# A two-block transformer kernel on one core: weights in pieces, products and vector steps in another order in five phases

## The chip, the cores and the metric

The program runs on one core of one Trainium2 chip. The metric is the device time of one execution in microseconds. Each engine of the core (TensorE or PE, VectorE or DVE, ScalarE or ACT, GpSimd or POOL) has its own instruction stream, and SyncE (SP) issues the DMA transfers. The streams meet only at semaphores. All data is float32. The trace has two rows for each float32 `matmul` of the code, while the listings of instruction order have one.

## The reference, cut to what matters

Two blocks are computed one after the other on 512 latent and 256 context tokens of width 1024. The first has two layers, each a mixer, a projection with a residual, and a gated feed-forward of width 2816. The second has a mixer of two branches and, at the end, a mixture of 16 experts in which each expert chooses its 64 tokens:

```python
m_lat = jnp.split((sc @ mod_w[l] + mod_b[l])[:, None, :], 6, axis=-1)      # modulation of a layer
h_lat = _modulate(_rms(x_lat, norm_pre_mix[l]), m_lat[0], m_lat[1])
...
x_lat = x_lat + m_lat[2] * _rms(o_lat @ w_out, norm_post_mix[l])           # the closing of a mixer
h_lat = _modulate(_rms(x_lat, norm_pre_ffn[l]), m_lat[3], m_lat[4])
x_lat = x_lat + m_lat[5] * _rms(_swiglu(h_lat, ...), norm_post_ffn[l])     # the tail of a feed-forward
...
affinity = jax.nn.softmax((h @ router_w).astype(F32), axis=-1)             # expert_choice_moe, 512 x 16
gate, idx = lax.top_k(jnp.swapaxes(affinity, 1, 2), cap)                   # cap = 64
xe = jax.vmap(lambda hb, ib: hb[ib])(h, idx)
hid = jax.nn.silu(xe @ w_gate) * (xe @ w_up)                               # for each expert, width 1408
ye = hid @ w_down * gate                                                   # added back at idx
```

## The kernel before

The program is a chain of phases. Each is a `Block` with its own semaphores, and each ends with a barrier over all engines, so nothing of a phase starts before the last instruction of the one ahead. Two things cross a barrier: data, and the object `Ahead`, a small buffer (`first`) into which the phase ahead has already loaded the first rows of the next phase's weights. Tokens come in six tiles of 128, two of context and four latent ones.

`opening` normalises and turns the six tiles and computes the first four blocks (of 512 columns) of layer 0's modulation. SP loads the tokens, the four blocks of weights of 2 MB each (line 236) and the tables (line 241). TensorE waits for each block and does 32 small products (8 slices `k`, 4 groups of columns; line 268). VectorE adds the bias (line 322), SP stores the result to memory (line 244) and loads it back as columns (lines 247 and 248), and then ScalarE and VectorE modulate all tiles.

`closing` runs three times: as `out0` (six tiles, weights ahead), `out1` (four tiles, none ahead) and `wo` (four tiles, weights ahead). It multiplies all tiles with weights in two jobs of 512 columns and eight slices `k`, then gates, adds to the residual, normalises and turns. Its unit is a tile of a job, summed over `k` in one bank of PSUM. Six banks are used in turn, and a unit beyond the sixth waits for `yg_done`. For job 0, slices 0 and 1 are in `ahead.tile`; slices 2 and 3, and then 4 to 7, are loaded at the start of the phase (`firsts`, line 402), and the first tile waits for each (`first_in`).

`down` (the second half of both feed-forwards) makes its products in pairs of tiles; the normalisation of a finished pair lies beside the next pair's products. For the last pair there is no next one, and its steps stand alone: ScalarE squares `y` (line 1068), VectorE takes the mean (`mean_y`), gates `y` (line 1158), takes the reciprocal (1160) and adds to `x` (`residual`, line 1163), ScalarE squares `x` (1077), VectorE takes the mean (`mean_x`) and scales (`normed`, lines 1173 and 1175), TensorE turns (line 1010), and ScalarE and VectorE (`take`) write the result.

`route` computes the logits (line 4284), the softmax and its transpose, and eight rounds of maximum search (lines 4329 and 4330) that mark each expert's 64 tokens in `taken`. A token's rank among those of its expert is a product with a triangle (`UPTO`) for its own tile and with ones for each tile before it (line 4300). From the ranks, VectorE writes `pick`, a 0/1 matrix of 512 tokens by 16 x 64 slots (line 4342). While this runs, SP fills the ring `experts_ring` with the first expert weights.

`experts` gathers the chosen tokens as products with `pick` (line 4409), by groups of 256 slots, that is four experts. Group 0 comes first, before anything else; the others are gathered as fillers between the products of a pair of experts. Line 4478 is the gate and up products, line 4511 the down products, line 4422 the scatter. Each piece of the ring that TensorE has used is released, and SP then loads the next piece into it (line 4636). VectorE begins the phase with the modulation (line 4544), waits for the row `gate` (line 4391), and multiplies `pick` with the gates (line 4559), which TensorE then turns (line 4417).

## Time and profile before

| what | us |
|---|---|
| runs of the kernel before | 4405.62, 4415.44, 4419.54 |
| their median | 4415.44 |
| the profiled execution, as timed | 4411.0 |
| its span in the trace | 4409.2 |
| TensorE busy | 4042.8 (92%) |
| VectorE busy | 1666.8 (38%) |
| ScalarE busy | 881.9 (20%) |
| GpSimd busy | 743.6 (17%) |

The span goes from the first to the last instruction in the trace; the time as measured has 1.8 us more around it. A line such as L465 names a line of the kernel. PE stands for products, PEld for the loading of the stationary operand, and SPq for the issue of transfers by SP. The granted clock (PEclk) is given as a share of 2.4 GHz, so 0.50 is 1.2 GHz. In the trace the parts of a tile's name before the first underscore are shortened: `out` is out0 and out1, `ffn_down` both layers.

### The profile page before, as it was taken

Reading aid. Unit: us, or ns where it says so; the run is one execution under the profiler, and the core shown is the slowest. Engines: PE = TensorE matmul, PEld = TensorE weight load, DVE = VectorE, ACT = ScalarE, POOL = GpSimd, SP = SyncE. Lnnn points to the kernel's source line nnn. Section 1 sums busy time; section 2 is a strip of 40 time slices with the busy share of each in tenths; the row PEclk is TensorE's granted clock in tenths of the full one; section 3 lists DMA queues with packets and bytes.
Section 4 is the critical chain, followed back from the end, with each engine's and each line's share of the span. In section 5 each row is a group of like instructions: output and inputs, shape, how many; then the busy total and the mean of one; then the engine's idle time right before and its main releaser. Section 6 shows DMA issues by size and latency. Waiting matters only on the chain. (4 is left out here: it accounts for less than half of the span.)

```text
span 4409.2 us, 46565 instructions
## 1 busy us (share of the span) xinstructions
PE 4042.8 (92%) x18631; PEld 2449.3 (56%) x18631; DVE 1666.8 (38%) x2942; ACT 881.9 (20%) x1666; POOL 743.6 (17%) x505
## 2 busy tenths in 40 slices
PE   7997889999989998899988999989998897999988
PEld 4664445554446765588546777775554445433433
DVE  2346342225724453433555566550024223111111
ACT  3124320000122333200013333321022211000000
POOL 0003212223411111123323333320002200000000
PEclk8999999999999999999999999999998997999999
DMA  4117511114421101353441000004200223899998
GB/s 167 39 43 261 169 40 64 64 43 148 170 84 29 53 29 59 117 209 116 144 117 29 22 27 20 17 32 142 70 1 1 108 84 126 361 421 421 422 421 369
DMA packets 317021, 579.68 MB, mean 131 GB/s; under 512 B 55836, under 2 KB 186108, under 8 KB 316168
## 3 DMA queue, kind: packets, MB, share of 16 engines
q1 hardware_dynamic: 316808, 576.70, 35.4%
q8 instruction: 150, 2.46, 0.2%
q14 instruction: 63, 0.52, 0.0%
HBM read 566.02 MB, written 10.63 MB: 131 GB/s over the span
## 5 line engine op out<-in xcount | busy, mean ns | idle before, releaser
L2951 PE MATMUL dn_ps<-room,dn_w 128*128 128x512 f32 (+1 forms) x616 | 226.1, 520 | 4.8 <-DVE dn_qx L3470 2.5
L764 PE MATMUL ffn_up_ps<-room,ffn_up_w 128*128 128x384 f32 (+1 forms) x704 | 209.0, 441 | 12.4 <-DMA ffn_up_w<-in_ffn_w_gate 12.4
L764 PE MATMUL ffn_up_ps<-ffn_up_t,room 128*128 128x384 f32 (+1 forms) x704 | 205.7, 436 | 0.8 <-DVE room L844 0.8
L764 PE MATMUL ffn_up_ps<-room 128*128 128x384 f32 (+1 forms) x704 | 203.9, 432 | 0.0
L4478 PE MATMUL experts_ps<-experts_ring,experts_xs 128*64 128x512 f32 (+1 forms) x768 | 165.3, 582 | 27.8 <-DMA experts_ring<-in_w_up 27.8
L2374 PE MATMUL hgrn_ps<-room,hgrn_w 128*128 128x512 f32 x384 | 175.2, 597 | 0.0
L764 PEld LDWEIGHTS ffn_up_ps<-room,ffn_up_w 128*128 128x128 f32 x704 | 135.2, 193 | 71.7 <-DMA ffn_up_w<-in_ffn_w_gate 13.2
L4478 PE MATMUL experts_ps<-experts_ring,room 128*64 128x512 f32 (+1 forms) x768 | 160.7, 570 | 8.7 <-DMA experts_ring<-in_w_up 8.1
L2951 PEld LDWEIGHTS dn_ps<-room,dn_w 128*128 128x128 f32 x616 | 116.3, 194 | 94.2 <-issue 81.7
L764 PEld LDWEIGHTS ffn_up_ps<-ffn_up_t,room 128*128 128x128 f32 x704 | 134.8, 192 | 57.6 <-DVE room L844 1.7
L4511 PE MATMUL experts_ps<-experts_ring,experts_hidT 128*64 128x512 f32 x704 | 155.0, 594 | 11.6 <-issue 6.9
L764 PEld LDWEIGHTS ffn_up_ps<-room 128*128 128x128 f32 x704 | 133.8, 190 | 55.7
L1039 PE MATMUL ffn_down_ps<-ffn_down_w_sums,ffn_down_hid_sums 128*128 128x512 f32 x330 | 161.7, 599 | 2.3 <-DVE ffn_down_w_sums L1127 2.3
L4554 DVE TENSOR_TENSOR x_sb<-x_sb,experts_ps 128x512 f32<-128x512 f32 x64 | 44.0, 688 | 300.3 <-PE experts_ps L4422 300.3
L851 DVE TENSOR_TENSOR room<-ffn_up_ps,room 128x384 f32<-128x384 f32 (+1 forms) x154 | 73.4, 489 | 222.2 <-PE ffn_up_ps L764 222.2
L3314 POOL TENSOR_TENSOR dn_LT<-dn_W,cst 128x768 f32<-128x768 f32 x48 | 90.6, 1887 | 340.6 <-DVE dn_W L3396 329.0
L2371 PE MATMUL hgrn_ps<-hgrn_w,room 128*128 128x384 f32 (+1 forms) x456 | 138.9, 453 | 3.1 <-DMA hgrn_w<-in_odd_w_in 3.1
L465 PE MATMUL out_ps<-out_w,room 128*128 128x512 f32 x296 | 134.4, 610 | 7.4 <-DMA out_w<-in_even_w_out 6.6
L4478 PEld LDWEIGHTS experts_ps<-experts_ring,experts_xs 128*64 128x64 f32 x768 | 59.1, 142 | 134.9 <-issue 131.7
L1039 PE MATMUL ffn_down_ps<-ffn_down_w,ffn_hid 128*128 128x512 f32 x220 | 116.3, 611 | 15.5 <-DMA ffn_down_w<-in_ffn_w_down 14.8
L822 POOL TENSOR_TENSOR room<-ffn_up_w 128x512 f32<-128x512 f32 x44 | 56.8, 1290 | 419.1 <-PE ffn_up_ps L764 233.0
L175 PE MATMUL in_ps<-in_w,room 128*128 128x512 f32 (+1 forms) x296 | 119.9, 565 | 0.3 <-DMA in_w<-in_w_in 0.3
(626 smaller groups left out, 7204.5 us busy)
## 6 DMA issues: line engine op xcount, KB each, us to landing
experts_ring<-in_w_gate SPq DMA_DIRECT2D x128, 704.0 KB, 15.8
experts_ring<-in_w_up SPq DMA_DIRECT2D x128, 704.0 KB, 17.8
experts_ring<-in_w_down SPq DMA_DIRECT2D x160, 512.0 KB, 14.5
ffn_down_w<-in_ffn_w_down SPq DMA_DIRECT2D x55, 1024.0 KB, 4.7
att_wm<-in_mod_w SPq DMA_DIRECT2D x20, 2048.0 KB, 8.9
ffn_up_wm<-in_ada_w SPq DMA_DIRECT2D x12, 2048.0 KB, 12.3
ffn_up_w<-in_ffn_w_up SPq DMA_DIRECT2D x22, 1024.0 KB, 7.7
ffn_up_w<-in_ffn_w_gate SPq DMA_DIRECT2D x20, 1024.0 KB, 5.3
```

What stands on the lines that cost most here:

```text
L175: mm = nc.tensor.matmul(ps[:, u % 8, 0:wd], xT[:, k, t * P:(t + 1) * P], ahead.tile[:, k, 0:wd] if j == 0 and k < n_ahead else wt[:, j % r ...
L465: mm = nc.tensor.matmul(ps[:, u % BANKS, 0:wd], xT[:, k, t * P:(t + 1) * P], ahead.tile[:, k, 0:wd] if j == 0 and k < n_ahead else wt[:, j ...
L764: mm = nc.tensor.matmul(result(n, p), lhs[:, k, :], rhs[:, k, :], start=k == 0, stop=k == half - 1)
L822: nc.gpsimd.tensor_tensor(s[:, 0, :, :], quarter(n, 1, lo), quarter(n, 1, hi), ALU.add).then_inc(S["s1_done"], 1)
L851: nc.vector.tensor_tensor(kept(n, to), result(n, p), kept(n, q), ALU.add).then_inc(done, 1)
L1039: mm = nc.tensor.matmul(result(p, prod), lhs, rhs, start=j == 0, stop=j == STEPS - 1)
L2371: mm = nc.tensor.matmul(ps[:, bank, 0:b - a], hT[:, k, t * P:(t + 1) * P], ahead.tile[:, k, :] if j == 0 and k < n_ahead else wt[:, s, k, ...
L2374: mm = nc.tensor.matmul(ps[:, bank, :], wt[:, s, k, piece * P:(piece + 1) * P], hT[:, k, CTX:], start=k == 0, stop=k == KD - 1)
L2951: mm = nc.tensor.matmul(out, ahead.tile[:, k, :] if k < by_ahead else wt[:, h % 2, piece, k, :], hT[:, k, tok], start=k == 0, stop=k == KD ...
L3314: nc.gpsimd.tensor_tensor(LT[:, :, :], W[:, h % 2, :, :], over_chunks(HALVES + n + 1), ALU.mult).then_inc(S["lt_done"], 1)
L4478: mm = nc.tensor.matmul(ps[out_rows, 3 * n + c, 0:b - a], xs_now[:, j, at:at + SLOTS], ring[:, w_at + a:w_at + b], start=j == 0, stop=j == ...
L4511: mm = nc.tensor.matmul(ps[out_rows, 6 + half, :], hidT[:, f, out_rows], ring[:, w_at:w_at + 512], start=f == 0, stop=f == FT - 1)
```

## The change

Five places change.

1. `opening` loads its last block of weights as four pieces of two slices `k`, each with its own semaphore, and TensorE waits for each piece where it needs it.
2. `closing` with weights ahead does the products of the slices at hand for all tiles first, into one bank for each tile, and then goes through the tiles with the remaining slices.
3. `down` interleaves the steps of its last two tiles on VectorE. The gating is now a function `gated` of its own; in the earlier pairs it is called right ahead of `residual`, as it stood.
4. `route` computes the ranks in four products in place of ten. The triangle is multiplied with `taken` of all four tiles at once, and the ones with `taken` of tiles 0 to 2, 0 to 1 and 0, each summed into the columns of the tiles behind.
5. `route` writes only the slots of group 0 (256 columns for each tile) of `pick`. The other 768 columns are written at the start of `experts`, behind VectorE's wait for the row `gate`; `slot` lives longer for it. VectorE's gating of a tile waits for `picked`, and so does TensorE ahead of the first gather of group 1.

```diff
@@ opening, SyncE and TensorE
             for b in range(blocks):
-                sp.dma_start(wt[:, b, :, :], mod.w[:, :, bass.ts(mod.b0 + b, 512)]).then_inc(S["w_in"][b], 16)
+                if b < blocks - 1:
+                    sp.dma_start(wt[:, b, :, :], mod.w[:, :, bass.ts(mod.b0 + b, 512)]).then_inc(S["w_in"][b], 16)
+                else:
+                    for n, (k0, k1) in enumerate(PIECES_OF_LAST):
+                        sp.dma_start(wt[:, b, k0:k1, :], mod.w[:, k0:k1, bass.ts(mod.b0 + b, 512)]).then_inc(S["last_in"][n], 16)
...
                 for k in range(KD):
+                    for n, (k0, k1) in enumerate(PIECES_OF_LAST):
+                        if b == blocks - 1 and k == k0:
+                            pe.wait_ge(S["last_in"][n], 16)
@@ closing, TensorE
+            if ahead:
+                wd = jobs[0][2]
+                pe.wait_ge(ahead.sem, 16)
+                for i, t in enumerate(tiles):
+                    for k in range(n_ahead):
+                        nc.tensor.matmul(ps[:, i, 0:wd], xT[:, k, t * P:(t + 1) * P], ahead.tile[:, k, 0:wd], start=k == 0, stop=False)
             for j, (v, c, wd, units) in enumerate(jobs):
...
-                    for k in range(kt):
+                    for k in range(0 if j else n_ahead, kt):
@@ down, VectorE, the end
-            last = finished_beside(n_pairs)
-            for t in last:
-                mean_y(t)
-            for t in last:
-                residual(t)
-            for t in last:
-                mean_x(t)
-                normed(t)
-            for t in last:
-                take(n_pairs, t)
+            one, other = finished_beside(n_pairs)
+            mean_y(one)
+            gated(one)
+            mean_y(other)
+            residual(one)
+            gated(other)
+            mean_x(one)
+            residual(other)
+            normed(one)
+            mean_x(other)
+            normed(other)
+            take(n_pairs, one)
+            take(n_pairs, other)
@@ route, TensorE and VectorE
-            for m in range(tiles):
-                for before in range(m + 1):
-                    mm = nc.tensor.matmul(ps[:, 3, m * E:(m + 1) * E], cst[:, UPTO[0], :] if before == m else ones, taken[:, before, :],
-                                          start=before == 0, stop=before == m)
+            flat = taken[:, :, :].rearrange("p m e -> p (m e)")
+            for later in range(tiles):
+                mm = nc.tensor.matmul(ps[:, 3, later * E:tiles * E], ones if later else cst[:, UPTO[0], :], flat[:, 0:(tiles - later) * E], start=later == 0, stop=later == tiles - 1)
...
-                by_slot = pick[:, m, :].rearrange("p (e s) -> p e s", e=E)
-                nc.vector.tensor_tensor(by_slot, ...
+                picks(nc, pick, slot, slot_iota, m, 0, GROUP)
+GROUP = 2 * P // SLOTS
@@ experts, TensorE
                     if what == "gather":
+                        if of == 1 and i == 0:
+                            pe.wait_ge(S["picked"], tiles)
@@ experts, VectorE
             dve.wait_ge(S["gate_in"], 16)
...
+            for m in range(tiles):
+                picks(nc, pick, slot, slot_iota, m, GROUP, EXPERTS).then_inc(S["picked"], 1)
+
             def gate_slots(m):
+                dve.wait_ge(S["picked"], m + 1)
```

On TensorE at the start of the closing `out0`, one row for each product (`first` is the buffer with the weights loaded ahead, `out_w` the weights loaded in the phase). Before:

```order
L465 MATMUL out_ps<-first,room 128x512 [waits first_odd_in]
L465 MATMUL out_ps<-first,room 128x512
L465 MATMUL out_ps<-out_w,room 128x512 [waits out0_first_in0]
L465 MATMUL out_ps<-out_w,room 128x512
L465 MATMUL out_ps<-out_w,room 128x512 [waits out0_first_in1]
L465 MATMUL out_ps<-out_w,room 128x512 x3
L465 MATMUL out_ps<-first,room 128x512 x2
L465 MATMUL out_ps<-out_w,room 128x512 x6
```

In the changed kernel:

```order
L460 MATMUL out_ps<-first,room 128x512 [waits first_odd_in]
L460 MATMUL out_ps<-first,room 128x512 x11
L478 MATMUL out_ps<-out_w,room 128x512 [waits out0_first_in0]
L478 MATMUL out_ps<-out_w,room 128x512
L478 MATMUL out_ps<-out_w,room 128x512 [waits out0_first_in1]
L478 MATMUL out_ps<-out_w,room 128x512 x33
```

Ten more products on `first` now stand ahead of the first wait for weights of the phase.

On VectorE from the end of `route` into `experts` (`slot_iota_sb` holds the slot numbers, `first` now holds the row `gate`, and `room` is where the gated picks go). Before:

```order
L4342 TENSOR_TENSOR pick<-slot_iota_sb,route_slot 128x1024 x3
L44 UNCONDITIONAL_BRANCH
L4541 UNCONDITIONAL_BRANCH [waits barrier_Pool_Activation_PE_DVE_SP_release]
L4544 SCALAR_TENSOR_TENSOR experts_mul<-experts_cols 128x8 [waits n0_ident_in0]
L4559 TENSOR_TENSOR room<-pick,gates 128x1024 [waits n0_cond_in0]
```

In the changed kernel:

```order
L4367 TENSOR_TENSOR pick<-slot_iota_sb,slot 128x256 x3
L44 UNCONDITIONAL_BRANCH
L4568 UNCONDITIONAL_BRANCH [waits barrier_Pool_Activation_PE_DVE_SP_release]
L4571 SCALAR_TENSOR_TENSOR experts_mul<-experts_cols 128x8 [waits n0_ident_in0]
L4367 TENSOR_TENSOR pick<-slot_iota_sb,slot 128x768 [waits n0_cond_in0]
L4367 TENSOR_TENSOR pick<-slot_iota_sb,slot 128x768 x3
```

Three quarters of the columns moved from ahead of the barrier to behind it. (A semaphore's number is used again by later phases, so the names in the brackets are those of its first user.)

## Rows read from the trace of the kernel before

**Rows 1.** The chain that ended last, from the page: shares by engine.
```profile
PE 10%; DMA 3%; SPq 2%; issue 0%; DVE 0%; ACT 0%; DVEq 0%
```

**Rows 2.** Timeline of the opening: start us, length us, engine, line, operation, [idle before].
```profile
29.95 2.62 PE L268 MATMUL n_ps<-n_w,conditions 128*2 128x128 f32 x64 [3.16 <-DMA n_w<-in_mod_w]
...
35.00 3.30 PE L268 MATMUL n_ps<-n_w,conditions 128*2 128x128 f32 x64 [2.43 <-DMA n_w<-in_mod_w]
...
39.59 1.18 SPq L244 DMA_DIRECT2D mod<-n_mod  x4
```

**Rows 3.** Transfers, 0 to 50 us: issues, KB each, us to landing.
```profile
cst<-in_tables SPq DMA_DIRECT2D x1, 1216.0 KB, 17.6
```

**Rows 4.** Timeline of TensorE at the start of the closing out0.
```profile
509.41 1.95 PE L465 MATMUL out_ps<-first,room 128*128 128x512 f32 x4 [1.10 <-PEq L47]
...
513.27 1.98 PE L465 MATMUL out_ps<-out_w,room 128*128 128x512 f32 x4 [1.91 <-DMA out_w<-in_even_w_out]
...
519.90 6.70 PE L465 MATMUL out_ps<-out_w,room 128*128 128x512 f32 x8 [4.64 <-DMA out_w<-in_even_w_out]
...
526.43 1.88 PE L465 MATMUL out_ps<-first,room 128*128 128x512 f32 x4
...
533.30 1.88 PE L465 MATMUL out_ps<-first,room 128*128 128x512 f32 x4
```

**Rows 5.** Stretches: length, busy time of five engines, granted clock, DMA share, GB/s.
```profile
519.90:523.00 3.10, 3.10 (x4) 1.50 (x5) 0.00 (x0) 0.00 (x0) 0.00 (x0) 0.50 1.06 371
...
2265.00:2275.00 10.00, 9.82 (x26) 4.24 (x24) 6.04 (x12) 0.59 (x1) 0.00 (x0) 1.00 0.00 1
```

**Rows 6.** Timeline of TensorE at the start of the closing wo.
```profile
3622.97 1.96 PE L465 MATMUL wo_ps<-first,room 128*128 128x512 f32 x4 [1.44 <-PEq L47]
...
3629.21 3.70 PE L465 MATMUL wo_ps<-wo_w,room 128*128 128x512 f32 x8 [0.99 <-DMA wo_w<-in_w_o]
...
3632.75 1.88 PE L465 MATMUL wo_ps<-first,room 128*128 128x512 f32 x4
```

**Rows 7.** Timeline of the tail of `down`, second feed-forward.
```profile
2277.77 0.15 DVE L1154 TENSOR_SCALAR first<-first 128x1 f32<-128x1 f32 x1 [1.31 <-ACT room L1068]
...
2279.16 1.28 DVE L1163 SCALAR_TENSOR_TENSOR x_sb<-room,first,x_sb 128x1024 f32<-128x1024 f32 x1
...
2280.37 1.22 DVE L1158 TENSOR_TENSOR room<-room,ffn_down_gate 128x1024 f32<-128x1024 f32 x1
...
2283.51 0.75 DVE L1175 TENSOR_SCALAR room<-x_sb,first 128x1024 f32<-128x1024 f32 x1
...
2284.41 3.31 PE L1010 MATMUL ffn_down_ps<-cst,room 128*128 128x128 f32 x16 [9.59 <-DVE room L1175]
```

**Rows 8.** Timeline of the routing phase.
```profile
3692.68 13.81 PE L4284 MATMUL route_ps<-first,room 128*128 128x16 f32 x64 [2.31 <-PEq L47]
...
3708.24 1.01 PE L4290 MATMUL route_ps<-cst_small,gates 128*16 128x128 f32 x4 [1.75 <-DVE gates L4324]
...
3727.89 0.22 DVE L4338 TENSOR_TENSOR route_slot<-route_ps,route_taken 128x64 f32<-128x64 f32 x1 [4.62 <-PE route_ps L4300]
...
3728.38 4.63 DVE L4342 TENSOR_TENSOR pick<-slot_iota_sb,route_slot 128x1024 f32<-128x1024 f32 x4
```

**Rows 9.** Timeline of the first feed-forward's `down`, one operation of VectorE.
```profile
1138.74 0.42 DVE L1117 TENSOR_TENSOR ffn_down_hid_sums<-ffn_hid 128x256 f32<-128x256 f32 x1
```

**Rows 10.** Timeline of the start of the experts' phase.
```profile
3733.73 17.40 PE L4409 MATMUL experts_ps<-pick,room 128*128 128x256 f32 x64 [5.95 <-PEq L47]
...
3739.49 2.36 DVE L4559 TENSOR_TENSOR room<-pick,gates 128x1024 f32<-128x1024 f32 x2 [1.84 <-DMA first<-mod]
...
3756.75 0.33 SPq L4636 DMA_DIRECT2D experts_ring<-in_w_gate  x1
```

**Rows 11.** Transfers, 3690 to 3760 us: GB/s in 40 slices of 1.75 us, and one issue.
```profile
GB/s 0 0 139 128 409 422 431 415 431 422 428 418 428 425 425 422 425 425 425 425 418 100 0 0 0 14 21 279 2 0 0 0 0 0 0 0 0 0 61 328
...
first<-mod SPq DMA_DIRECT2D x1, 512.0 KB, 4.5
```

**Rows 12.** Transfers, 3760 to 4409 us: GB/s in 40 slices of 16.2 us.
```profile
GB/s 319 400 410 419 424 423 422 419 421 423 424 422 419 421 422 425 420 420 418 425 422 423 419 420 423 422 424 418 420 423 422 424 419 418 424 423 423 420 360 130
```

More of the change, by code:

```diff
@@ L464, in _ @@
                                 pe.wait_ge(S["first_in"][n], 16 * (len(v[k0 >= kt // 2]) if type(v) is tuple else 1))
-                        mm = nc.tensor.matmul(ps[:, u % BANKS, 0:wd], xT[:, k, t * P:(t + 1) * P], ahead.tile[:, k, 0:wd] if j == 0 and k < n_ahead else wt[:, j % ring, k, 0:wd], start=k == 0, stop=k == kt - 1)
+                        mm = nc.tensor.matmul(ps[:, u % BANKS, 0:wd], xT[:, k, t * P:(t + 1) * P], wt[:, j % ring, k, 0:wd], start=k == 0, stop=k == kt - 1)
                     mm.then_inc(S["mm_done"], 1)
@@ L4248, in quarter_tables, with route @@
     return {name: np.ascontiguousarray(t.astype(np.float32)) for name, t in tables.items()}
-def route(nc, tag, hT, I, cst, ones, slot_iota, pick, aff, work, load, places, ahead):
+def route(nc, tag, hT, I, cst, ones, slot_iota, slot, pick, aff, work, load, places, ahead):
     tiles = TILES - CTX_TILES
@@ L4340, in _, with picks, experts @@
             for m in range(tiles):
-                by_slot = pick[:, m, :].rearrange("p (e s) -> p e s", e=E)
-                nc.vector.tensor_tensor(by_slot, slot_iota[:, 0:SLOTS].unsqueeze(1).broadcast_to([P, E, SLOTS]),
-                                        slot[:, m, :].unsqueeze(2).broadcast_to([P, E, SLOTS]), ALU.is_equal)
-def experts(nc, tag, x, x_hat, pick, aff, gated, pick_gateT, gain, mod, w_gate, w_up, w_down, ident, ring, load, piece_in, places, pool, xs, hid, hidT, gate, out):
+                picks(nc, pick, slot, slot_iota, m, 0, GROUP)
+GROUP = 2 * P // SLOTS
+def picks(nc, pick, slot, slot_iota, m, e0, e1):
+    shape = [P, e1 - e0, SLOTS]
+    return nc.vector.tensor_tensor(pick[:, m, e0 * SLOTS:e1 * SLOTS].rearrange("p (e s) -> p e s", s=SLOTS), slot_iota[:, 0:SLOTS].unsqueeze(1).broadcast_to(shape),
+                                   slot[:, m, e0:e1].unsqueeze(2).broadcast_to(shape), ALU.is_equal)
+def experts(nc, tag, x, x_hat, slot, slot_iota, pick, aff, gated, pick_gateT, gain, mod, w_gate, w_up, w_down, ident, ring, load, piece_in, places, pool, xs, hid, hidT, gate, out):
     F, FT = EXPERT_FF, EXPERT_FF // P
@@ L4383, in experts @@
         phase(nc, tag, "cols_in", "gate_in", "mul_done", "piece_used", "up_mm", "silu_done", "hid_done", "turned", "hid_turned", "down_mm", "out_done",
[L4384 removed]
+              "gather_mm", "gather_out", "picked", "gated_done", "pick_turned", "pick_taken", "scatter_mm", "scatter_out", "stored") as (block, S),
     ):
```

21 lines of the change are left out of this document (11 added, 10 removed).

## The prediction

> **What bounds the kernel now.** I read four views in this order. The chain that ended last covers 15% of the span, which is the experts' phase alone (from 3733 us on): 10% is TensorE and 5% transfers of the ring and their issue [rows 1]. The transfers move 418 to 425 GB/s in every full slice from 3809 us to 4376 us [rows 12], so that stage goes by its transfers, and what it costs as a whole is fixed by bytes. What is not fixed is when it begins. Before 3733 us the program is a row of phases with a barrier behind each, so a microsecond taken from the path inside a phase is a microsecond of the span, unless something inside that phase is then late. So I read, second, the timelines of the five places that the change touches and looked for what the last instruction of each phase had waited for; third, the granted clock of TensorE there; fourth, the transfers around the routing phase. All sums are against the profiled execution: 4409.2 us span, 4411.0 us as timed. That is 4.4 us under the median of 4415.4 us, so the predicted time is the median less the gain.
>
> **Opening.** The last 2 MB of weights land at 35.00 us, 5.05 us behind the third block, and only then do 32 products run (64 rows of the trace, two for each float32 product) in 3.30 us [rows 2]. In four pieces the first three land some 1.25, 2.5 and 3.8 us behind the third block's and are used before the last lands, for 16 rows of the trace need at most 0.83 us. Left behind 35.00 us is one piece, 3.30 / 4 = 0.83 us. Saved: 2.5 us. What could be late next is the table load. It is queued right behind these weights with 1216 KB [rows 3]; at the rate of the weights (2 MB in 5.05 us) it needs 3.0 us and lands at 38.0 us. It used to be done when the modulation was stored at 39.59 us [rows 2]. The stores now start 2.5 us earlier, at 37.1 us, and overlap its last microsecond. I take 0.1 us off for that: 2.4 us, between 1.6 (the stores wait for all of the table) and 2.5.
>
> **Closing of layer 0 (out0).** TensorE does four trace rows on the weights loaded ahead, waits, does four on the first piece, waits 4.64 us for the second, and does the next eight in 6.7 us at a granted clock of 0.50, which is 1.2 GHz [rows 4, 5]. Tile 0 takes 526.43 - 509.41 = 17.02 us; tile 1, with nothing to wait for, takes 533.30 - 526.43 = 6.87 us, or 0.429 us a row. The loss is 10.15 us. In the changed kernel 24 rows on the weights at hand come first and take 24 x 0.429 = 10.3 us, to 519.7 us. The first piece landed by 513.27 us and is at hand. Its four rows end at 521.4 us, and the second piece landed by 519.90 us. Neither wait is left, and TensorE is busy all the while, so I take the clock to stay at 2.4 GHz. What is next late? Tile 0's product ends at about 525 us instead of 526.4; job 1 starts at 550.6 instead of 560.8 us and needs the bank of tile 0, free by 528 us, and weights issued before 521 us. Nothing. Saved: 10.1 us. The bounds: 6.9 us if the eight rows still run at 1.2 GHz (then 3.2 us stays lost), 10.2 at most.
>
> **Closing of block 2 (wo).** The same with four tiles: 3632.75 - 3622.97 = 9.78 us for tile 0 against 6.87 [rows 6], a loss of 2.9 us. The 16 rows on weights at hand take 6.9 us, to 3629.9 us; the second piece landed by 3629.21 us. Saved: 2.9 us, bounds 2.3 (the two waits alone) and 2.9. The third closing (out1) has nothing loaded ahead and does not change.
>
> **Tail of `down`, in both feed-forwards.** VectorE's order is now by dependence rather than by kind. In the profile of before, VectorE stands idle for 1.31 us until ScalarE's second square is done, at 2277.77 us, and only then gates the first tile (1.22 us, as the second's at 2280.37); the first normalised tile starts at 2283.51 [rows 7]. Now the first gating lies in that idle stretch, from 2276.5 us. The first residual starts at 2278.0, the second gating at 2279.2, ScalarE's square of the first x at 2279.4, and the second residual at 2280.8. The first normalised tile starts at 2282.2, which is 1.3 us earlier; the second is 1.0 us earlier. TensorE's 16 transposes start at 2284.41 [rows 7] and then run without a gap worth naming, so the first tile sets the end. I take 1.2 us each, 2.4 us for two, with bounds 1.6 and 2.6. The cover here is VectorE's idle stretch; if ScalarE's square were quicker, the gating would be on the path again.
>
> **Routing.** Ranks: VectorE waits 4.62 us for 20 trace rows of TensorE [rows 8]. The 64 logit rows of the same phase and width take 13.81 / 64 = 0.216 us each, so the 20 are 4.3 us of it, and 0.3 us is fixed. Now there are eight rows, with 64, 48, 32 and 16 columns. The wider ones are new; four transposes of the same phase move 128 columns and take 1.01 / 4 = 0.25 us a row, which bounds them. I take 8 x 0.216 = 1.7 us. Saved: 2.6 us, bounds 2.3 and 2.6. Picks: four operations of 1024 columns take 4.63 us [rows 8]. Four of 256 columns remain: at least 4.63 / 16 = 0.29 us each by columns, at most 0.42 us as a 128x256 operation in `down` lasts [rows 9]. I take 0.35, 1.4 us together. Saved: 3.2 us, bounds 2.95 and 3.5. The gather and with it the whole ring schedule start 5.8 us earlier.
>
> The other 768 columns go to the start of the experts' phase, behind the wait for the gate, which ended 5.8 us into that phase [rows 10]: 4 x 0.87 = 3.5 us (three quarters of 4.63), over 9.3 us in. Queued behind them on VectorE is the gating of the picks for the transposes, which TensorE takes up only after its first gather of group 1. TensorE's own new wait stands at that gather, which begins with the first release of the ring at 3756.75 us, 23 us in [rows 10]. So the added work lies beside other work with 13 us to spare. Without that cover it would cost 3.5 us.
>
> **Sum.** 2.4 + 10.1 + 2.9 + 2.4 + 5.8 = 23.6 us. 4411.0 - 23.6 = 4387.4 us against the profiled execution, 4391.8 us against the median: 4392 us, ratio 0.9947. With all low bounds it is 17.7 us, with all high ones 24.3.
>
> **Two rules against the trace.** In the profile of before, transfers of 512 and 704 KB in the ring keep about 422 GB/s as long as several are queued [rows 11, 12]. The Trainium skill, "DMA: Bandwidth & Descriptors", section "Bandwidth", asks instead for transfers of 1 MiB and more and gives about three quarters of peak at that size; by an estimate from its fit (2 us fixed and bytes over 436 GB/s), three more transfers would cost 6 us if they stood one behind the other, and the opening would lose 3.5 us. The trace disagrees for queued transfers; no run so far shows it in the opening. Second, in `down` TensorE changes its PSUM bank after every two trace rows for a whole stage at a granted clock of 1.00 [rows 5]. The Trainium skill, "TensorE: Matmul & The Clock Gate", section "A second HAM failure mode: psum-queue depth-cycling", warns that cycling through banks each iteration can make the clock swing. The new loop in out0 changes banks after every four rows, so by the rule the clock could fall there; the trace speaks against it.
>
> **Rivals.**
> (a) *The routing's gain is taken back by the ring.* If the transfers of the experts' stage were already under way without a break, starting TensorE earlier would move nothing: 4392 + 5.8 = 4398 us. Against it: the rate falls to 0 at about 3728 us, with the ring full, and rises only when the first pieces are released at 3756.75 us [rows 10, 11]. The release moves with the gather.
> (b) *The clock stays low in out0* while the banks are cycled: 24 + 12 rows at twice 0.429 us cost 15 us more, which leaves a gain of 8 us: 4407 us. Against it is the stretch of `down` [rows 5].
> (c) *The opening's pieces run one behind another.* A 512 KB load of the gate row lands 4.5 us after its issue [rows 11]; four of them in a row would need 18 us instead of 5: 4392 + 13 = 4405 us. The Trainium skill's fit above is the mild form of this rival. Against it is the queued rate.
> (d) *Slower: the new wait on `picked` stalls the ring.* If the gate's load were queued behind ring pieces, VectorE would come late to the 768 columns, TensorE would stand at the first gather of group 1, and with it every release behind it. It costs nothing up to 23 us into the phase, and a microsecond for each one after that; it eats the whole gain from 23 + 23.6 = 46.6 us on, where I work out 9.3. Picks that end 60 us in would give 4392 + 37 = 4429 us. What speaks for it is only that the phase now starts at 3727.9 us, within a microsecond of the ring's last first-fill piece.
> (e) *The change doesn't do what it says* at one place (a wait that I take as gone has another cause, out0's being the large one): 4392 + 6 = 4398 us.
>
> **Chances.** Forecast 0.78; (a) 0.06; (b) 0.03; (c) 0.02; (d) 0.03; (e) 0.08. The runs of before spread from 4405.6 to 4419.5 us, so a median of three may be 5 us off by itself, about as much as the bounds of the sum leave open. Forecast alone: 4385 to 4400 us. With (a), (e) and half of the rest: 4381 to 4404 us. About 0.3% (13 us) is what a measurement of this kernel can tell from no change: faster by more than that is 0.86 (forecast, (a), (e), less the noise), within it 0.11 ((b), (c) and noise), slower 0.03 ((d)).
>
> **What would show it.** In the changed profile: out0's first 24 rows without a gap and clock 1.00 throughout job 0, tile 0 ending near 525 us less the opening's 2.4; the opening's last block in four groups of products, 0.8 us of them behind the last landing; the rank products within 2 us; the experts' first gather 5.8 us earlier relative to the routing's start, and the first ring release 23 us after it as before; no wait of TensorE on VectorE's picks. The prediction is wrong if TensorE's clock is low in out0, if the ring's rate in the experts' stage is not the one of before, or if the stage's length from gather to end is not the same.

## The result, and the profile after

| what | before | changed |
|---|---|---|
| median, us | 4415.29 | 4390.03 |
| runs, us | 4405.62 to 4419.54 (4) | 4389.81 to 4390.7 (4) |
| ratio of the runs, 95% interval | | 0.9946 (0.9929 to 0.9963) |
| the profiled execution, as timed | 4411.0 | 4390.07 |
| its span | 4409.2 | 4388.3 |
| TensorE busy | 4042.8 | 4037.8 |

The changed kernel is faster by 25.3 us by the medians and by 23.8 us by the means, where 23.6 us had been forecast; the ratio in the table is that of the means. Between the two profiled executions it is 20.9 us. The rest of this document compares traces, and so explains the 20.9 us. The difference to 25.3 comes from where the two profiled executions stand among their runs: the one of the kernel before is 4.3 us under its median, and the one of the changed kernel is on its median.

*The page.* The chain that ended last has the same makeup as in [rows 1], and the experts' stage moves data at the same rate as in [rows 12]. Shares by engine, and GB/s from 3739 to 4388 us in 40 slices:

```profile
PE 11%; DMA 3%; SPq 1%; issue 0%; DVE 0%; ACT 0%; DVEq 0%
...
GB/s 312 403 416 419 425 422 423 419 421 422 424 422 418 421 422 424 421 420 420 422 423 424 419 419 423 426 421 420 418 423 424 423 419 419 423 424 422 420 348 129
```

*Opening.* Timeline of the changed kernel, to set beside [rows 2]. The last column is the idle time ahead of the group and what ended it.

```profile
29.92 4.91 PE L277 MATMUL n_ps<-n_w,conditions 128*2 128x128 f32 x112 [4.06 <-DMA n_w<-in_mod_w]
...
35.01 0.62 PE L277 MATMUL n_ps<-n_w,conditions 128*2 128x128 f32 x16 [0.18 <-DMA n_w<-in_mod_w]
...
36.91 1.18 SPq L249 DMA_DIRECT2D mod<-n_mod  x4
```

The third block (64 rows) and three of the four pieces (48 rows) now form one group of 112, with no gap that the trace sets apart. One piece of 16 rows is left behind the last landing at 35.01 us. The four pieces land in the time of the one transfer (35.00 us before). The store is issued 2.68 us earlier.

*Closing of layer 0.* TensorE, as [rows 4]:

```profile
508.95 10.54 PE L460 MATMUL out_ps<-first,room 128*128 128x512 f32 x24 [1.10 <-PEq L47]
519.32 51.23 PE L478 MATMUL out_ps<-out_w,room 128*128 128x512 f32 x119
```

Both waits are gone: 119 rows follow on the 24 without a gap. The granted clock is 1.00 over both jobs; the one stretch at 0.50 in this phase begins at 600.7 us, when they are done. Three stretches (length, PE busy, clock, DMA share, GB/s):

```profile
505.00:515.00 10.00, 8.23 (x30) 1.00 0.50 122
515.00:520.00 5.00, 5.00 (x13) 1.00 1.03 272
520.00:525.00 5.00, 5.00 (x13) 1.00 1.09 367
```

*Closing of block 2.* TensorE from the end of the phase ahead, as [rows 6], and below it a stretch with the same columns:

```profile
3605.76 0.66 PE L4160 MATMUL mix_ps<-cst,mix_sum 128*128 128x128 f32 x4 [1.07 <-DVE mix_sum L4248]
3607.86 8.80 PE L460 MATMUL wo_ps<-first,room 128*128 128x512 f32 x16 [1.44 <-PEq L47]
3616.49 8.75 PE L478 MATMUL wo_ps<-wo_w,room 128*128 128x512 f32 x20
...
3608.20:3611.20 3.00, 3.00 (x4) 0.50 0.75 253
```

Here too the waits are gone, but 16 rows take 8.80 us instead of 6.9: for some 3 us the granted clock is 0.50.

*Tail of `down`, second feed-forward*, as [rows 7]:

```profile
2268.57 0.15 DVE L1167 TENSOR_SCALAR first<-first 128x1 f32<-128x1 f32 x1 [0.62 <-ACT room L1081]
2268.64 1.21 DVE L1170 TENSOR_TENSOR room<-room,ffn_down_gate 128x1024 f32<-128x1024 f32 x1
...
2271.49 1.22 DVE L1170 TENSOR_TENSOR room<-room,ffn_down_gate 128x1024 f32<-128x1024 f32 x1
...
2274.44 0.75 DVE L1190 TENSOR_SCALAR room<-x_sb,first 128x1024 f32<-128x1024 f32 x1
...
2275.34 3.65 PE L1023 MATMUL ffn_down_ps<-cst,room 128*128 128x128 f32 x16 [8.27 <-DVE room L1190]
```

TensorE's idle time ahead of the transposes falls from 9.59 to 8.27 us, 1.3 us less. The first gating lies directly behind the first mean, in what was idle time.

*Routing*, as [rows 8]:

```profile
3691.95 1.01 PE L4308 MATMUL route_ps<-cst_small,gates 128*16 128x128 f32 x4 [1.75 <-DVE gates L4341]
...
3707.03 0.69 PE L4318 MATMUL route_ps<-route_taken,cst_small 128*128 128x64 f32 x2 [0.32 <-DVE route_taken L4350]
...
3707.51 1.41 PE L4318 MATMUL route_ps<-route_taken,ones_sb 128*128 128x48 f32 x6
3709.03 0.23 DVE L4355 TENSOR_TENSOR slot<-route_ps,route_taken 128x64 f32<-128x64 f32 x1 [2.06 <-PE route_ps L4318]
...
3709.52 1.43 DVE L4367 TENSOR_TENSOR pick<-slot_iota_sb,slot 128x256 f32<-128x256 f32 x4
```

VectorE waits 2.06 us for the ranks instead of 4.62, and its picks take 1.43 us instead of 4.63: 2.56 and 3.20 us.

*Start of the experts' phase*, as [rows 10]:

```profile
3711.68 17.95 PE L4434 MATMUL experts_ps<-pick,room 128*128 128x256 f32 x64 [2.76 <-PEq L47]
...
3716.64 3.56 DVE L4367 TENSOR_TENSOR pick<-slot_iota_sb,slot 128x768 f32<-128x768 f32 x4 [2.31 <-DMA first<-mod]
...
3735.16 4.21 PE L4434 MATMUL experts_ps<-pick,room 128*128 128x256 f32 x16
3735.25 0.33 SPq L4667 DMA_DIRECT2D experts_ring<-in_w_gate  x1
```

The 768 columns are done at 3720.2 us, 8.5 us behind the start of the first gather. TensorE's first gather of group 1, 15 us later, has no idle time ahead of it. The first release is 23.6 us behind the first gather (23.0 before).

### The profile page after: what moved, and what is told of

It reads as the page before. It is cut to its first block and busy times, and to the rows that moved or that the text cites. A ratio compares the mean times of both kernels' runs of the same rounds, so it can differ in the third digit from the quotient of the medians.

```text
span 4388.3 us, 46552 instructions
## 1 busy us (share of the span) xinstructions
PE 4037.8 (92%) x18619; PEld 2443.9 (56%) x18619; DVE 1668.8 (38%) x2946; ACT 882.0 (20%) x1666; POOL 743.0 (17%) x505
```

## The experiments

Each phase ends with a barrier, so the traces can be compared phase by phase. The table stands for all that follows. It gives the length of a phase from barrier to barrier in us, and in brackets how much of it lies at a granted clock of 0.50. The numbers are worked out from the barrier ends and clock records of each trace.

```
phase          before      before      parts 1 to 4 of the change alone            changed kernel
                           again       opening    ahead      tail       route      first      again      third
opening       49.4(18)    49.9(17)    47.1(13)   49.6(17)   50.7(18)   49.4(18)   46.7(16)   47.9(15)   46.7(13)
att, block 0 198.4(38)   200.4(41)   202.0(44)  198.0(38)  198.0(38)  203.1(51)  201.1(44)  201.1(44)  197.4(34)
out0         107.2(12)   105.3(10)   106.7(12)   97.1( 6)  104.8( 9)  106.5(15)   97.1( 5)   97.1( 5)   97.1( 5)
down0        227.4(21)   226.9(21)   227.3(21)  227.0(21)  225.8(17)  227.3(21)  226.0(17)  226.1(17)  226.0(17)
hgrn         483.6(13)   483.4(16)   483.6(17)  483.3(16)  484.7(17)  483.6(17)  484.7(17)  484.9(17)  484.8(17)
out1          94.3(22)    94.2(22)    94.4(22)   97.7(29)   98.2(32)   94.2(22)   98.2(32)   94.6(25)   98.1(32)
down1        161.2(21)   161.3(21)   161.4(23)  161.2(21)  160.2(21)  161.2(21)  160.9(21)  160.0(21)  159.8(21)
dn           709.8(40)   706.6(33)   709.5(41)  703.7(24)  707.6(37)  703.7(24)  708.1(36)  707.5(37)  707.6(36)
mla          364.2(64)   360.4(53)   363.4(60)  363.2(59)  360.5(53)  363.2(59)  360.2(53)  360.2(53)  360.2(53)
mix          127.0( 3)   127.1( 3)   127.0( 3)  125.7( 0)  127.1( 3)  127.0( 3)  125.9( 0)  127.1( 3)  127.0( 3)
wo            69.7( 6)    69.7( 6)    69.7( 6)   68.5(10)   69.6( 6)   69.7( 6)   68.5( 7)   66.8( 6)   66.8( 6)
route         41.1(41)    41.1(41)    41.1(41)   41.1(41)   41.1(41)   35.3(35)   35.3(35)   35.3(35)   35.3(35)
experts      675.5(30)   676.3(39)   677.1(25)  676.1(31)  675.8(32)  675.3(27)  676.6(38)  677.7(37)  677.0(42)
all phases  4408.9      4401.1      4409.9     4391.2     4403.8     4400.1     4387.9     4387.0     4384.1
```

(The four phases left out, `gla`, `up0`, `up1` and `in2`, stay within 1.7 us of each other over all nine.)

### One part of the change alone

Each kernel is the one before with the lines of one part of the diff shown ahead of the prediction: part 1; part 2; part 3; parts 4 and 5.

> The kernel before with the opening's last weights in pieces and nothing else. My theory: the opening ends 2.7 us earlier (46.7 instead of 49.4 us, as in the changed kernel), and the phases whose code is the same move by up to 4 us each, up or down, because the granted clock falls at other places in them; so the total is 2.7 us less, give or take 5: 4407 to 4417 us against 4415. Rival, parts add up exactly and the other phases stay put: every phase behind the opening has its length of before to 0.3 us and the total is 4412.6 us.

Measured: 4405.55 us (4403.68 to 4415.56, 10 runs), ratio 1.0 (0.9991 to 1.001). The opening is 47.1 us long, against 49.4 to 50.7 in the five traces with the old one: at least 2.3 us less. Part of that spread is the landing itself, for the last weights land between 34.8 and 36.1 us in those five and at 35.33 us here. From the first product on the last weights to the end of the phase it is 14.7 to 14.9 us in the five and 12.0 us here, so 2.6 to 2.9 us less. The rival, that the other phases stay put to 0.3 us, is refuted: `att` is 3.6 us longer and `mla` 0.8 us shorter.

> The kernel before with the products on the weights at hand first, in both closings. My theory: out0 is 10.1 us shorter in this run too, its 24 first rows at a granted clock of 1.00. In wo the changed kernel gave only 1.2 us because half of the 16 rows ran at 1.2 GHz; if that was where the clock happened to fall, wo gives 1.2 to 2.9 us here and its 16 first rows take 6.9 or up to 10.5 us. Rival: going from bank to bank brings the clock down, then the 16 rows of wo take 8.8 us here too, and the 24 rows of out0 show a low clock in some part. Total 4400 to 4407 us by either.

Measured: 4397.58 us (4390.5 to 4405.16, 9 runs), ratio 0.9981 (0.9971 to 0.999). `out0` is 97.1 us long. The old one takes 104.8 to 107.2 in five traces, so the gain is 7.7 to 10.1 us. `wo` is 68.5 instead of 69.7, and its 16 first rows take 8.80 us: 1.2 us where 2.9 was forecast, as in the first trace of the changed kernel. That is half of the rival's sign; the other half, a low clock in the 24 rows of `out0`, is missing. The banks get a test of their own below.

> The kernel before with the interleaved tail of the last pair. My theory: from the first mean of y to the first product of the next phase 12.4 and 12.6 us instead of 13.9 and 13.6, so 2.5 us in all, and the total 2.5 us less, give or take the clock's 5: 4408 to 4418 us. Rival: the earlier transposes run at a lower clock and give the gain back, then the two stretches are 13.3 us or longer and the total does not move.

Measured: 4410.77 us (4401.75 to 4412.91, 10 runs), ratio 1.0006 (0.9996 to 1.0015). The interval reaches from 1.8 us less to 6.6 us more and does not contain the 2.5 us that were expected, though the two phases are shorter, by 1.1 to 1.6 and by 1.0 to 1.2 us.

> The kernel before with the ranks in four products and the picks by group. My theory: the routing phase is 35.3 us instead of 41.1, the first gather starts 5.8 us earlier and the experts' phase keeps its length of 675.5 us to 0.5, so the total is 5.8 us less, give or take the clock's 5 in earlier phases. Rival: the experts' phase takes some of it back, since it was 1.1 us longer in the changed kernel (676.6), then it is again 676.6 us here.

Measured: 4402.88 us (4396.52 to 4408.94, 10 runs), ratio 0.9993 (0.9984 to 1.0002). The routing is 35.3 us instead of 41.1, 5.8 as worked out, and the experts' phase has kept its length (675.3 against 675.5 to 677.1).

The kernel before has a median of 4407.39 us on that chip (4399.86 to 4416.89, 30 runs). The four differences of medians are 1.8, 9.8, -3.4 and 4.5 us, 12.7 together, while the changed kernel wins 25.3 and, below, 21.9. Each of the four has an interval of some 4 us to both sides, so the medians can't say what a part of 2 us is worth, and whether the missing 9 us are more than noise stays open. In the traces the parts do add up: over the phases that they touch, the four kernels are 2.3, 11.3, 2.6 and 5.8 us shorter than the first trace of the kernel before, 22.0 together, and the changed kernel in its first trace 21.5. What follows from these four runs is read phase by phase in the table.

*Where the tail's gain went.* One row of the table answers it. The phase behind the first feed-forward, `hgrn`, isn't touched by the diff. It takes 483.3 to 483.6 us in all five traces with the old tail and 484.7 to 484.9 in all four with the new one. Its first products on TensorE, in the kernel before:

```profile
1244.35 3.65 PE L1010 MATMUL ffn_down_ps<-cst,room 128*128 128x128 f32 x16 [9.59 <-DVE room L1175]
1250.19 2.90 PE L2371 MATMUL hgrn_ps<-first,room 128*128 128x384 f32 x4 [2.19 <-PEq L47]
1256.19 5.83 PE L2371 MATMUL hgrn_ps<-hgrn_w,room 128*128 128x384 f32 x12 [3.10 <-DMA hgrn_w<-in_odd_w_in]
```

And in the changed kernel:

```profile
1232.48 3.47 PE L1023 MATMUL ffn_down_ps<-cst,room 128*128 128x128 f32 x16 [8.27 <-DVE room L1190]
1238.13 2.02 PE L2390 MATMUL hgrn_ps<-first,room 128*128 128x384 f32 x4 [2.19 <-PEq L47]
1243.81 6.83 PE L2390 MATMUL hgrn_ps<-hgrn_w,room 128*128 128x384 f32 x12 [3.66 <-DMA hgrn_w<-in_odd_w_in]
```

The same 12 rows take 1.0 us more. The stretch around them stands at 0.72 before and at 0.50 after (length, busy time of five engines, clock, DMA share, GB/s; kernel before, then changed):

```profile
1254.80:1261.00 6.20, 4.81 (x10) 2.68 (x11) 1.65 (x10) 0.23 (x1) 0.00 (x0) 0.72 0.86 150
```

```profile
1242.80:1249.00 6.20, 5.19 (x8) 2.86 (x9) 1.65 (x10) 0.23 (x1) 0.00 (x0) 0.50 0.95 173
```

The clock records say when. In all five traces with the old tail TensorE stands at 0.50 when `hgrn` begins, and the last low stretch at its start ends 9.4 to 9.8 us into the phase. In all four with the new tail the clock is back at 1.00 across the barrier, falls 1.0 us into the phase and stays low until 11.2 to 11.4 us. The first 16 rows of `hgrn` are done 0.7 to 1.2 us later for it, counted from the phase's start, and some 0.4 us more are lost around a second low stretch, which begins at 71 us with the old tail and at 73 with the new one. Why the clock falls there at all with the new tail isn't shown.

`down0` and `hgrn` together are 710.3 to 711.0 us in the five traces with the old tail and 710.5 to 711.0 in the four with the new one. So the 1.1 to 1.6 us that the first tail wins are given back in the next phase, in the form of a later stretch at 1.2 GHz. Behind the second tail, `dn` moves by up to 6 us in traces with the same tail (703.7 to 709.8), so whether that gain survives can't be told.

### The same kernels again

> The changed kernel once more, beside runs of the kernel before on the same chip, and its trace. My theory (run-to-run spread comes from where the granted clock falls): its runs spread over some 15 us as those of the kernel before do, their median lies 17 to 25 us below it, and in the trace att0, out1, dn and mla, whose code is unchanged, differ from the first trace by 2 to 6 us each, each with its time at 1.2 GHz. Rival, the changed kernel is tied to one good alignment: 4390 us again within 1 us, and the same phase lengths to 0.3 us.

Measured: 4384.6 us (4383.82 to 4390.21, 5 runs) against 4406.45 (4399.25 to 4419.09, 11 runs), ratio 0.9953 (0.9937 to 0.9968): 21.9 us. `out0` and `route` are as in the first trace, `wo` is 66.8 us, and `out1`, which is the same code as before, falls back from 98.2 to 94.6. Of the four phases that I had named, only `out1` moved as expected; `att` and `mla` are the same to 0.1 us and `dn` differs by 0.6, and the runs spread over 6.4 us and not 15. So neither theory holds whole: phases do move between executions, but fewer than I thought. The 25.3 us of the first comparison also rest on four runs of the kernel before with a median of 4415.29 us, while the 41 later ones, beside the kernels of this section and the one ahead of it, have medians of 4407.39 and 4406.45.

> The changed kernel, unchanged, profiled a third time. Asked: is the last product of block 2 (68.5 us in the first trace, 66.8 us in the second) set by where the clock falls. If so, its 16 products between the turns take 7.1 us with the granted clock at 1.00 over them or 8.8 us with a stretch at 0.50, and the stage 66.8 or 68.5 us accordingly, nothing else. If the second trace was special for another reason, some third value. Query product of block 0 97.1 us and routing 35.3 us as in both traces; sum within 10 us of 4387 us.

> The kernel before, unchanged, profiled a second time. Asked: how far the stages of one and the same code move between two executions. If where the granted clock falls is drawn anew in each execution, single stages (attention of block 0, the query product of block 1, the network and attention of block 2) will stand 1 to 5 us from the first trace, each together with its own time at the 1.2 GHz level, with a sum within some 10 us of 4408.9 us; the stages with little time at 1.2 GHz within 0.5 us. If it follows from the code alone, each stage agrees with the first trace within 0.5 us. Of the changed places: query product of block 0 between 104.8 and 107.2 us, last product of block 2 69.7 us, routing 41.1 us.

Measured, on one chip: 4386.21 us, and 4403.19 us for the kernel before, 17.0 apart; one more run of the kernel before beside them took 4409.73 us, 23.5 above. In the third trace of the changed kernel the 16 rows of `wo` run at full clock:

```profile
3603.16 0.66 PE L4160 MATMUL mix_ps<-cst,mix_sum 128*128 128x128 f32 x4 [1.07 <-DVE mix_sum L4248]
3605.26 7.11 PE L460 MATMUL wo_ps<-first,room 128*128 128x512 f32 x16 [1.44 <-PEq L47]
...
3605.30:3612.00 6.70, 6.70 (x16) 3.08 (x17) 0.00 (x0) 0.00 (x0) 0.00 (x0) 1.00 0.85 303
```

The idle times ahead of them (1.07 and 1.44 us) are the same to the hundredth as in the first trace, where 8.80 us stood. Where the low stretch went is seen in the phase ahead, `mix`. Third trace:

```profile
3526.05 1.94 PE L4150 MATMUL mix_ps<-cst,room 128*128 128x128 f32 x8 [2.57 <-ACT mix_yT L4200]
...
3525.60:3529.00 3.40, 2.94 (x10) 2.44 (x11) 3.33 (x5) 1.97 (x4) 0.00 (x0) 0.51 0.00 0
```

First trace, at the same place of the phase:

```profile
3530.07 1.12 PE L4150 MATMUL mix_ps<-cst,room 128*128 128x128 f32 x8 [2.71 <-ACT mix_yT L4200]
...
3528.40:3531.80 3.40, 1.73 (x10) 1.30 (x11) 3.02 (x5) 2.23 (x5) 0.00 (x0) 1.00 0.00 0
```

In every one of the nine traces one stretch of 3.4 us at 0.50 lies either in `mix`, where it costs 1.1 to 1.4 us, or right at the start of `wo`, where TensorE is never idle and it costs 1.7. Over both phases the gain is 2.8 to 3.0 us in two traces of the changed kernel (193.9 and 193.8 against 196.7 and 196.8), and 2.3 in the first (194.4). What decides between the two places isn't shown.

The second trace of the kernel before moves the same way: `att` +2.0, `out0` -1.9, `dn` -3.2, `mla` -3.8 us, and 7.8 us in all, with not a letter of the code changed. `out1`, which I had expected to move as well, is the same to 0.1 us. With the old `out0`, the eight rows on the late weights are at 1.2 GHz for a longer or shorter part of their length. 6.70 us in [rows 4] is this in the second trace:

```profile
520.75 5.39 PE L465 MATMUL out_ps<-out_w,room 128*128 128x512 f32 x8 [4.06 <-DMA out_w<-in_even_w_out]
```

### Does changing the bank cost clock?

The loop over the weights at hand, with tiles and slices exchanged, so that the bank changes with each product instead of every second one:

```diff
-                for i, t in enumerate(tiles):
-                    for k in range(n_ahead):
+                for k in range(n_ahead):
+                    for i, t in enumerate(tiles):
```

> The changed kernel with the products on the weights at hand taken slice by slice instead of tile by tile, so that each one goes to another bank than the one before. The same products and sums. My theory: the granted clock follows what TensorE did before, not the banks: the 24 rows of out0 take 10.5 us again, the 16 of wo 6.9 to 10.5 us with the low part at their beginning. Rival (the Trainium skill, TensorE: Matmul & The Clock Gate, section A second HAM failure mode: psum-queue depth-cycling): changing banks lets the clock swing, then changing twice as often gives more of it: over 12 us for the 24 rows, over 9 us for the 16.

Measured: 4391.65 us (4386.17 to 4396.4, 7 runs), ratio 0.996 (0.9946 to 0.9974). `out0` is 97.1 us and `wo` 66.8 us long, as in the second and third trace of the changed kernel. The 24 rows of `out0` and the clock over them:

```profile
514.03 10.54 PE L460 MATMUL out_ps<-first,room 128*128 128x512 f32 x24 [1.10 <-PEq L47]
...
514.00:524.30 10.30, 10.27 (x24) 4.67 (x25) 0.00 (x0) 0.00 (x0) 0.00 (x0) 1.00 0.86 227
```

So neither the clock nor the length of these phases depends on how often the bank changes here. The rule of the Trainium skill that the prediction weighed ("TensorE: Matmul & The Clock Gate", section "A second HAM failure mode: psum-queue depth-cycling") isn't borne out at this place, and the bank isn't what made `wo` slow in the first trace. The page tells of a bfloat16 kernel whose TensorE idles briefly between groups of products; the 24 rows here are float32 and have no gap between them, so that case isn't tested.

The whole kernel was slower than the changed kernel beside it, by 7.0 us in the median and 4.4 in the mean, with ranges that overlap. Its trace is 2.7 us longer than the second one of the changed kernel, and 4.0 us of difference lie in `att` (205.1 us, 58 of them at 0.50, against 201.1), which runs ahead of the edited loop. Whether the rest is more than noise wasn't measured.

### Keeping TensorE busy

If low stretches give gains back, products whose results nobody reads might prevent them. The first kernel puts four behind the last two turns of `wo` and eight beside the maximum search of the routing; the second also puts seven of 384 columns into the tail of `down`:

```diff
+            for n in range(SLOTS // 8):
+                pe.wait_ge(S["own"], 4 + 2 * n)
+                nc.tensor.matmul(ps[:, 4, 0:BUSY], cst[:, IDENT, :], hT[:, 0, 0:BUSY], start=True, stop=True)
             pe.wait_ge(S["mask_done"], 1)
```

> The changed kernel with products whose results nobody reads: four in the idle stretches of TensorE at the end of wo, and eight of 512 columns beside the eight rounds of the maximum search. My theory: the routing runs at 1.2 GHz only because TensorE stood idle before it. With the idle filled, the 64 logit rows take 6.9 instead of 13.8 us, the ranks about 1 instead of 2.1, the first gather 16.6 instead of 17.9, and wo is not longer: routing 27 to 29 us instead of 35.3, total 7 to 9 us below the changed kernel. Rival: the logit rows are bound by their weight loads or by issue and not by the clock, then they stay at 13.8 us and nothing moves.

Measured: 4386.5 us (4382.88 to 4388.25, 4 runs), ratio 0.9953 (0.9936 to 0.997), the same as the changed kernel beside it. The routing is 33.6 us long, 1.7 less. I had expected 27 to 29 us, and 7 to 9 us off the total. The 64 logit rows, which I had expected at full clock, are not:

```profile
3673.43 13.06 PE L4314 MATMUL route_ps<-first,room 128*128 128x16 f32 x64 [1.45 <-PEq L47]
...
3673.40:3674.00 0.60, 0.57 (x6) 1.00 0.00 0
3674.00:3675.00 1.00, 1.00 (x8) 0.62 0.48 139
3675.00:3676.00 1.00, 1.00 (x6) 0.50 0.37 97
```

`wo` now has no low stretch at all, but the clock falls one microsecond into the logits, behind the 1.4 to 1.5 us of idle time at the barrier and with TensorE busy without a gap. The six rows at 1.00 take 0.1 us each and the later ones 0.2, so the rival is wrong too: it is the clock that the rows go by. What the fillers keep up is the end of the phase: VectorE waits 1.23 us for the ranks instead of 2.06. The first gather behind it takes 17.7 us, where 16.6 was expected.

> As before this, and seven more such products of 384 columns in each tail of down, each behind a step of VectorE or ScalarE. My theory: the 16 transposes of each tail take 1.9 instead of 3.5 us and the next phase starts at 2.4 GHz, 1.5 to 3 us a tail, so 3 to 6 us less than the kernel with the busy routing alone. Rival: the transposes wait for VectorE's second tile anyway, and the next phase waits for its weights; then it gains less than 1.5 us, or the added products hold the first transpose up.

Measured: 4386.91 us (4382.76 to 4391.68, 4 runs), ratio 0.9955 (0.9937 to 0.9973). `down0` is 224.8 us (226.0 to 226.5 without the fillers), with 10.2 us at 0.50 instead of 17.1. Its 16 transposes take 1.2 us for each eight, at full clock, but with a wait of 0.57 us for VectorE's second tile between them, as the rival had it. `hgrn` is 485.0 us: no less than in the changed kernel. The low stretch at its start is there all the same, and over the two phases the fillers bring about 1 us (709.8 against 710.5 to 711.0 in the three traces of the changed kernel and the one of its tail alone). The 24 rows of `out0` had a low stretch in this execution (12.23 us, phase 98.8), the only one of seven with the new loop. Neither version is measurably faster than the changed kernel.

## Why the prediction was right

| term | forecast, us | measured at its place | what became of it |
|---|---|---|---|
| opening | 2.4 | 2.7 (2.3 with this part alone) | kept, 1.5 in the second trace |
| `out0` | 10.1 | 10.1 against the first trace | 7.7 to 10.1 against five |
| `wo` | 2.9 | 1.2 | 2.9 in the other two traces |
| tails | 2.4 | 2.5 (1.5 and 1.0) | the first given back in `hgrn` |
| routing | 5.8 | 5.8 | kept |
| sum | 23.6 | 22.3 | 20.9 as timed |

**Opening, ranks and picks.** The three costs that were taken from rows of the trace came out within 0.3 us. Of the opening's 3.30 us, 0.62 is left rather than 0.83, because that piece ran at a granted clock of 1.00, while the clock was 0.57 over the 3.30 us. The 0.1 us for the table load was not needed: the store is issued as soon as the bias is added. In the second trace of the changed kernel the pieces' products run at 1.2 GHz, one behind another without a gap, and the phase takes 47.9 us; there the cover is thinner than I worked out, and the gain is 1.5 us against the first trace of the kernel before.

**`out0`.** The step held as written: 24 rows in 10.54 us, no wait, full clock. The gain was sized on one execution, however. The old phase depends on how much of the eight rows behind its 4 us wait is at 1.2 GHz, and the first trace happened to have the longest: 107.2, where the mean of five is 106.1. The new phase is 97.1 us in six of the seven traces that have it. That most of the variation would go with the wait wasn't foreseen.

**`wo`.** This is the term that was mis-sized in the first trace: 1.2 instead of 2.9. The waits went as told. The failed step is "the 16 rows on weights at hand take 6.9 us", which priced them at full clock: they took 8.80 us, some 3 of them at 0.50. The idle time ahead of the phase would not have told, for it is the same in the third trace, where they take 7.11 us. The same step is right in two other traces. What the prediction lacked is a bound for a low stretch falling on these rows: its low bound of 2.3 us is above the 1.2 us measured.

**Tails.** The order of steps and the 1.2 us each are right (1.5 and 1.0). What failed is the silent assumption that the phase behind keeps its length. It cost 1.1 to 1.6 us in `hgrn` in every trace with the new tail. "What is next late" was asked inside the phase only, and of waits only. So of this term's 2.4 us the first half is worth nothing in the total.

**Experts.** 676.6 against 675.5 us in the first pair; 675.3 to 677.1 in the six traces of the kernel before and of one part alone, and 676.6 to 677.7 in the three of the changed kernel. The prediction had named a change of this length as a sign that it is wrong; the 676.6 us of the first trace lie within the spread of the other six, the 677.7 of the second 0.6 us above it. Half of the 1.1 us is in the first gather, 17.95 against 17.40 us [rows 10], and that half is the clock's. The first gather of `route` alone and of the changed kernel's second trace, each with its first 6.5 us (length, busy time of five engines, clock, DMA share, GB/s):

```profile
3725.16 16.94 PE L4415 MATMUL experts_ps<-pick,room 128*128 128x256 f32 x64 [2.76 <-PEq L47]
3725.20:3731.70 6.50, 6.50 (x22) 5.92 (x23) 1.88 (x3) 1.13 (x2) 0.00 (x0) 0.76 0.26 85
```

```profile
3709.60 18.16 PE L4434 MATMUL experts_ps<-pick,room 128*128 128x256 f32 x64 [2.75 <-PEq L47]
3709.60:3716.10 6.50, 6.50 (x17) 5.42 (x18) 1.71 (x3) 0.56 (x1) 0.00 (x0) 0.54 0.29 85
```

The low stretch of the routing goes on 3.2 to 6.1 us into this phase. Over the nine traces of the table the gather's length follows from that alone: 16.9 us with 3.2 us at 0.50, 17.4 with 4.3, 17.95 with 5.6, 18.2 with 6.1. The picks are not the cause: `route` alone writes them too and has the shortest gather, and no engine waits for them. What is left of the phase is 658.5 to 659.5 us in the changed kernel and 658.0 to 659.6 in the other six.

**The total.** 22.3 us at the places; less 0.8 in the rest of `down0` and `down1`, less 1.1 in `experts`, and 0.6 more in phases that the diff doesn't touch make the 21.0 us between the two spans. That 0.6 is what is left of phases that became longer and shorter: +2.7 (`att`), +3.9 (`out1`), -4.0 (`mla`), -1.7 (`dn`) and smaller ones, among them the +1.1 of `hgrn`. The forecast of 4392 us hit 4390 since two errors worked against each other: the traces gave 2.7 us less than the sum, and the place of the profiled execution under its median gave 4.4 us more. The mechanisms at the five places were right; that the time agrees to 2 us is partly luck.

**The rivals.** (a) Ring takes the gain back: refuted, the first release moved with the gather, and the routing alone keeps its 5.8 us. (b) Low clock in `out0`: in six of the seven traces with the new loop there is none in the 24 rows; in the seventh there are 1.7 us of it, where the rival had 15. (c) Pieces one behind another: refuted, they land when the single transfer did, at 35.01 us. The fit of the Trainium skill ("DMA: Bandwidth & Descriptors", section "Anatomy of one DMA — SWDGE (gpsimd) path") is given there for single transfers issued by GpSimd; for these four, queued by SyncE, a fixed part for each isn't borne out. (d) Wait on `picked`: the picks end 8.5 us behind the start of the gather (9.3 worked out), and TensorE comes for them after 23.5. (e) One place fails: none did; `wo` came nearest.

## What to carry to other kernels

Put the products whose operands are already there ahead of the first wait, for all tiles and not only for the first; beside the wait it also removes the low clock behind it, and the phase then had the same length, 97.1 us, in six of seven traces. When a step is taken out of a phase's tail, look at the granted clock at the start of the phase behind: in this kernel the microsecond won in front of one barrier was lost behind it. Take a second trace of the unchanged kernel before explaining phases by a few microseconds, since here the same code differed by 7.8 us in all and by up to 3.8 in one phase.

## What the runs showed of the hardware

- Two executions of one kernel agree to 0.1 us in phases such as `route`, and can differ by 2 to 4 us in `att`, `out1`, `dn` and `mla` (`out1` 98.2 and 94.6 us with 32 and 25 us at 0.50, `mla` 364.2 and 360.4 with 64 and 53), each together with the time that it spends at 0.50.
- A stretch at 1.2 GHz can start when TensorE has just taken up work without a gap (at the start of `wo`, and one microsecond into the logits), behind idle times of 1.1 to 1.5 us. It need not: behind the same idle times the 16 rows of `wo` took 8.80 us once and 7.11 another time.
- A low stretch goes on across a barrier: the routing's reached 3.2 to 6.1 us into the experts' phase and made its first gather 16.9 to 18.2 us long.
- Busy time is not the cure by itself: in the routing the fillers saved 1.7 us of 35.3, though 11 us of the phase then stood at 2.4 GHz where none had.
- Changing the PSUM bank with each product cost these rows nothing (10.54 us for the 24 of `out0` both ways).
- Four queued transfers of 512 KB land as early as one of 2 MB (35.01 and 35.00 us in the first pair; 34.9 to 36.3 and 34.8 to 36.1 over all traces that show the landing).
